# Opening stage of a diffusion trunk layer: conditioning product turned round, modulated tile in PSUM

## The chip, the cores and the metric

One core of one Trainium2 chip runs the kernel. The metric is the device time of one execution in microseconds (us). The kernel before took 2195.75 us in the median of three runs (2195.32 to 2199.14).

## The reference

One trunk layer runs on 1024 latent and 128 context tokens of 1024 channels in fp32. What matters here is its beginning:

```python
mod = silu(cond) @ ada_w + ada_b            # cond: two vectors (latent, context); ada_w is 1024 x 6144
sh1, sc1, g1, sh2, sc2, g2 = split(mod, 6)
h = rms_norm(x, n1_pre) * (1 + sc1) + sh1   # rms_norm: x * rsqrt(mean(x*x) + eps) * n1_pre
proj = h @ w_in                             # 1024 x 8192
```

After that come retention, a convolution branch, a merge and a convolutional feed-forward part. None of them is touched.

## The kernel before

A product in fp32 precision is made of three fp32r products: each operand is split into a high part (`A_hi`, `Wa_hi`) and a rest (`A_lo`, `Wa_lo`), and hi x hi, hi x lo and lo x hi are summed in PSUM. ScalarE makes the high part of a weight chunk (`split_w`) and GpSimd the rest.

All orders are written out by hand, one program for each engine, with semaphores between them. The opening stage goes so:

- SyncE loads `x` in three groups of three 128-token tiles, `ada_w`'s first 2048 columns in eight pieces of 256 columns (`ada_chunk`, 1 MB each), small rows, and chunks of `w_in` (`chunk_load`, 512 KB each), in one queue.
- TensorE multiplies each piece by the two conditioning vectors (`ada_early`): `cs` is the stationary operand (two columns), the piece moves. The result lies as two rows in PSUM. VectorE copies them to `mod_row` (`row_half`, L2188) and TensorE turns them into columns (`mod_turns`, L990, 16 turns of 2x128). VectorE adds the bias (`mod`) and forms `hscale`. The last piece comes behind the first eight of these turns and two `x_turn`.
- ScalarE squares the token tiles (`square`, L1450) and takes roots (`root`), VectorE forms the mean (`meaned`) and scales `x_all` (`normed`, L2184). In ScalarE's queue the squares of group 0 and 1 stand ahead of all modulated tiles, those of group 2 behind tile 7.
- There are 24 steps j = 8 g + k, one for each token group g (384 tokens) and 128-channel block k. TensorE turns three x tiles into one of three PSUM banks (`x_turn`, L1004). ScalarE scales and shifts the bank into one of six SBUF tiles `hf` (`modulated`, L1467). VectorE makes `A_hi` (L2197) and `A_lo` (L2198) from it (`halves`). In six of the steps ScalarE makes `A_hi` itself (`ON_ACT`).
- `first_u` on TensorE takes the 24 steps as they come: for each g first slot e = 0, whose step k waits for `A_lo` of j, then e = 1. `ahead` says how many `x_turn` stand ahead of each step. Behind it comes `q_half(0)`, the first product with 512 moving columns.

From step 3 on an `x_turn` waits until ScalarE has emptied the bank, and ScalarE's tile j waits for VectorE's j - 6, which frees its `hf` tile. Later in the kernel `ada_part` multiplies the other pieces of `ada_w` with the piece as stationary operand, strewn between other products. TensorE's products all have line L953, the helper `mm`.

Of the kernel before, what the change touches and what calls it, by code (L numbers as in the profile page):

```python
# [6 lines left out]
P = 128  # L7
D = 1024
# [55 lines left out]
def build(nc, a, out_xp, out_xs, out_sf, out_sb):  # L64
# [8 lines left out]
    with ctx:  # L73
# [56 lines left out]
        mod_row = at("mod_row", [2, 2 * D], a_at + 8 * KT * 2 * P * 4)  # L130
# [30 lines left out]
        hf = s0("hf", [P, 6, TG])  # L161
# [434 lines left out]
        ON_ACT = lambda j: j < 2 * KT and j % KT % 3 == 1  # L596
# [39 lines left out]
        def _(sp):  # L636
# [73 lines left out]
            ada_chunk(7)  # L710
            x_load(1)
            chunk_load(1)
# [238 lines left out]
        def _(pe):  # L951
# [28 lines left out]
            def ada_early(n):  # L980

                pe.wait_ge(ada_in[n % 4], 16 * (n // 4 + 1))
                for k in range(KT):
                    last = mm(ps[0:2, n // 2, (n % 2) * 256:(n % 2 + 1) * 256], cs[:, k, :], ada_p[:, n, k, :], k == 0, k == KT - 1)
                return last
            def mod_turns(half):

                pe.wait_ge(q.vec_ok, (2, 8)[half])
                for m in range(8 * half, 8 * half + 8):
                    pe.transpose(ps[:, 6, 2 * m:2 * m + 2], mod_row[0:2, m * P:(m + 1) * P], ident[0:2, 0:2]).then_inc(q.ada_used, 1)  # L990
            def x_turn(j):

                g, k = divmod(j, KT)
                if j == 0:
                    pe.wait_ge(q.vec_ok, 7)
                if j == 2:
                    pe.wait_ge(q.mod_ok, 1)
                if j >= 3:
                    pe.wait_ge(q.hT_f, j - 2)
# [17 lines left out]
            for n in range(8):  # L1017
                if n == 4:
                    row_turns()
                if n == 7:  # L1020
                    mod_turns(0)
                    x_turn(0)
                    x_turn(1)
                last = ada_early(n)
                if n % 4 == 3:
                    last.then_inc(q.vecT, 1)
            mod_turns(1)
            x_turn(2)


            def first_u():

                turned = 3
                pe.wait_ge(q.vec_ok, 8)
                for g in range(NTG):
                    for e in range(2):
# [6 lines left out]
                        for k in range(KT):  # L1043
                            ahead = KT * g + (k + 4 if e == 0 else 11 + (k // 2 if g else 0))
# [372 lines left out]
        def _(act):  # L1417
# [37 lines left out]
            def modulated(j):  # L1455
# [3 lines left out]
                if j >= 6:  # L1459
                    act.wait_ge(q.hT_lo, j - 5)  # L1460
                src, n = ps[:, TURN_BANK[j % 3], 0:TG], TG if g < 2 else 2 * P
                t3 = lambda x: x.rearrange("p (t n) -> p t n", n=P)
                outs = [t3(hf[:, j % 6, :])]
                if ON_ACT(j):
                    outs.append(A_hi[:, 3 * g:3 * g + 3, k, :])
# [7 lines left out]
            def squares(g):  # L1473

                for t in range(3 * g, 3 * g + 3):
                    square(t)
                root(g)
            squares(0)
            split_w(0)
            squares(1)  # L1480
            act.wait_ge(q.mod_ok, 2)
            for j in range(N_A):
                modulated(j)
                if j == 7:
                    squares(2)
                if j in (3, 15, 19, 21, 23):
                    split_w((3, 15, 19, 21, 23).index(j) + 1)
# [641 lines left out]
        def _(dve):  # L2129
# [55 lines left out]
            def row_half(n):  # L2185

                dve.wait_ge(q.vecT, (2, 8)[n])
                dve.tensor_copy(mod_row[:, n * D:(n + 1) * D].rearrange("c (b n) -> c b n", b=2),  # L2188
                                ps[0:2, 2 * n:2 * n + 2, :]).then_inc(q.vec_ok, 1)
            def halves(j):  # L2190
# [3 lines left out]
                h_ = hf[:, j % 6, :].rearrange("p (t n) -> p t n", n=P)  # L2194
# [9 lines left out]
            row_half(0)  # L2204
            dve.wait_ge(q.vecT, 7)
# [3 lines left out]
            row_half(1)  # L2209
            meaned(1)  # L2210
            dve.wait_ge(q.ada_used, 16)
            dve.wait_ge(q.vec_ok, 3)
            dve.tensor_tensor(mod[:, 0:16, :], ps[:, 6, 0:32].rearrange("p (k c) -> p k c", c=2), col2(V_ADAB, 16),
# [4 lines left out]
            for j in range(N_A):  # L2218
                if j == 3:
                    normed(1)  # L2220
                if j == 8:
                    meaned(2)
                    normed(2)
# [486 lines left out]
```

## Time and profile before

| | |
|---|---|
| median of the runs | 2195.75 us |
| the profiled execution | 2197.59 us |
| its span | 2195.8 us |
| TensorE busy (matmul) | 2142.4 us, 98% |
| VectorE / ScalarE / GpSimd busy | 1589.4 / 788.1 / 966.9 us |
| mean granted TensorE clock | 0.993 |

The profiled execution lies 1.8 us above its span. PE is the matmul side of TensorE, PEld its weight loads, DVE is VectorE, ACT is ScalarE, POOL is GpSimd, SP is SyncE. The granted clock is a share of 2.4 GHz; 0.50 is 1.2 GHz. The ends of matmuls are modelled, so the distance between two starts says more than a busy time.

### The profile page before, as it was taken

What the parts mean: (1) busy time and instruction counts of PE and PEld (TensorE: products, weight loads), DVE (VectorE), ACT (ScalarE), POOL (GpSimd) and SP (SyncE); (2) the same over time, 40 slices, a digit from 0 to 9 for tenths busy, and PEclk for the clock granted to TensorE, in tenths of its full rate; (3) what the DMA queues carried; (4) which work ended last, traced back from release to release, by engine and by line L of the source; (5) the groups of instructions that cost most, each with busy time, mean ns of one, the idle gap of its engine ahead of it and who ended that gap; (6) DMA issues with size and microseconds to landing.
All of it is one profiled execution on the core that took longest, in us unless ns stands there. A gap on an engine that the chain in (4) does not pass through costs nothing.

```text
span 2195.8 us, 31594 instructions
## 1 busy us (share of the span) xinstructions
PE 2142.4 (98%) x12483; PEld 1965.5 (90%) x12483; DVE 1589.4 (72%) x1790; ACT 788.1 (36%) x1326; POOL 966.9 (44%) x619
## 2 busy tenths in 40 slices
PE   7999999999999899999999999999999999999998
PEld 3888988988988899999899988889999999978886
DVE  3689589589489467676436536699898988766775
ACT  3401101101101266665548333343343333434342
POOL 1323323323323356665381220056656656565653
PEclk9999999999999999999999999999999999999999
DMA  9342442442432445545464344313232323375553
GB/s 304 111 128 95 129 128 87 133 128 81 131 106 88 156 153 164 167 147 158 153 219 146 125 168 141 99 35 87 63 88 61 91 61 91 107 296 183 201 181 128
DMA packets 246579, 291.79 MB, mean 133 GB/s; under 512 B 12225, under 2 KB 198945, under 8 KB 246433
## 3 DMA queue, kind: packets, MB, share of 16 engines
q1 hardware_dynamic: 178385, 221.33, 32.0%
q10 hardware_dynamic: 66640, 63.72, 8.9%
q0 software_dynamic: 1408, 4.72, 0.5%
q8 instruction: 100, 1.64, 0.3%
q14 instruction: 46, 0.38, 0.1%
HBM read 222.71 MB, written 67.01 MB: 132 GB/s over the span
## 4 chain that ended last, share of the span: by engine, by line
PE 90%; DVE 4%; DMA 2%; POOL 1%; ACT 1%; issue 1%; SPq 0%; ACTq 0%; DVEq 0%; POOLq 0%
PE ps L953 88%; DVE f_cv L2563 1%; DVE T_raw L2523 1%; PE ps L1163 1%; DMA ada_p<-in_ada_w 1%; DVE A_lo L2198 1%; POOL O_lo L2099 0%; DMA r_raw<-rT_d 0%; PE ps L1211 0%; DMA kv<-qkvg_d 0%; DMA sh_row<-gain_d 0%; DMA g_raw<-g_d 0%; DMA W_raw<-in_w_mix_out 0%; DVE A_hi L2197 0%; POOL f_cv L2104 0%
## 5 line engine op out<-in xcount | busy, mean ns | idle before, releaser
L2241 DVE SCALAR_TENSOR_TENSOR conv_y<-u_in,VC,conv_y 128x1167 f32<-128x1167 f32 x240 | 395.9, 1650 | 7.4
L1960 POOL TENSOR_TENSOR Wa_lo<-W_raw,Wa_hi 128x1024 fp32r<-128x1024 f32 x58 | 143.7, 2485 | 398.1 <-ACT Wa_hi L1419 398.0
L953 PE MATMUL ps<-A_hi,Wa_hi 128*128 128x384 f32 x768 | 271.8, 354 | 8.1 <-DVE A_lo L2198 7.3
L953 PE MATMUL ps<-A_hi,Wa_lo 128*128 128x384 f32 x768 | 259.6, 338 | 0.0
L953 PE MATMUL ps<-A_lo,Wa_hi 128*128 128x384 f32 x768 | 259.4, 338 | 0.0
L2563 DVE SCALAR_TENSOR_TENSOR f_cv<-f_in,VF,f_cv 128x1023 f32<-128x1023 f32 (+1 forms) x176 | 216.1, 1279 | 3.8 <-ACT f_cv L1847 2.1
L1960 POOL TENSOR_TENSOR D_lo<-F_raw,D_hi 128x1024 fp32r<-128x1024 f32 x66 | 162.3, 2463 | 100.0 <-ACT D_hi L1419 100.0
L2600 DVE TENSOR_TENSOR g_lo<-g_raw,g_hi 128x384 fp32r<-128x384 f32 x66 | 138.7, 2111 | 81.3 <-ACT g_hi L1419 81.3
L2099 POOL TENSOR_TENSOR O_lo<-E,O_hi 128x512 fp32r<-128x512 f32 x80 | 130.1, 1627 | 151.7 <-ACT O_hi L1419 151.7
L953 PE MATMUL ps<-Wb_hi,A_hi 128*128 128x512 f32 x432 | 179.7, 416 | 0.0
L2099 POOL TENSOR_TENSOR O_lo<-F_raw,O_hi 128x512 fp32r<-128x512 f32 x68 | 113.1, 1665 | 146.1 <-ACT O_hi L1419 146.1
L953 PE MATMUL ps<-Wb_hi,A_lo 128*128 128x512 f32 x432 | 170.7, 395 | 0.0
L953 PE MATMUL ps<-Wb_lo,A_hi 128*128 128x512 f32 x432 | 169.3, 392 | 0.0
L953 PE MATMUL ps<-D_hi,g_hi 128*128 128x512 f32 x396 | 155.2, 392 | 4.6 <-POOL D_lo L1960 2.4
L953 PEld LDWEIGHTS ps<-A_hi,Wa_hi 128*128 128x128 f32 x768 | 146.3, 190 | 11.5 <-DVE A_lo L2198 9.5
L953 PE MATMUL ps<-D_lo,g_hi 128*128 128x512 f32 x396 | 154.7, 391 | 0.0
L953 PE MATMUL ps<-D_hi,g_lo 128*128 128x512 f32 x396 | 154.6, 390 | 0.0
L1419 ACT ACTIVATE Wa_hi<-W_raw 128x1024 fp32r<-128x1024 f32 x58 | 60.6, 1056 | 259.2 <-DVE qk_st L2267 152.2
L953 PEld LDWEIGHTS ps<-A_lo,Wa_hi 128*128 128x128 f32 x768 | 146.3, 191 | 0.8
L953 PEld LDWEIGHTS ps<-A_hi,Wa_lo 128*128 128x128 f32 x768 | 145.6, 190 | 0.0
L953 PE MATMUL ps<-T_hi,O_hi 128*128 128x288 f32 x640 | 138.1, 298 | 4.5 <-ACT f_in L1419 4.0
L953 PE MATMUL ps<-B_hi,O_hi 128*128 128x288 f32 x608 | 140.9, 296 | 1.5 <-DVE B_lo L2509 1.0
(291 smaller groups left out, 5608.2 us busy)
## 6 DMA issues: line engine op xcount, KB each, us to landing
F_raw<-in_ffn_w_down SPq DMA_DIRECT2D x66, 512.0 KB, 3.6
F_raw<-in_ffn_w_up SPq DMA_DIRECT2D x44, 512.0 KB, 5.9
qt<-qkvg_d SPq DMA_DIRECT2D x36, 512.0 KB, 3.8
W_raw<-in_w_in SPq DMA_DIRECT2D x32, 512.0 KB, 5.1
W_raw<-in_w_in SPq DMA_DIRECT2D x64, 256.0 KB, 3.2
ada_w<-in_ada_w ACTq DMA_DIRECT2D x30, 512.0 KB, 4.3
g_d<-f_cv SPq DMA_DIRECT2D x22, 576.0 KB, 3.6
g_raw<-g_d SPq DMA_DIRECT2D x66, 192.0 KB, 3.6
```

The costliest lines, as they stand in the source:

```text
L953: return pe.matmul(out, l, r, start=start, stop=stop)
L1163: last = pe.transpose(ps[:, 2, x * P:(x + 1) * P], qt[:, n % 5, x // 2, (x % 2) * P:(x % 2 + 1) * P], ident[:, :])
L1419: return act.activation(dst, src, ACT.Copy)
L1960: return pool.tensor_tensor(dst, x, Fv(hi), ALU.subtract)
L2099: pool.tensor_tensor(O_lo[o % 4][:, :, :], op_src(o)[2], Fv(O_hi[o % 4][:, :, :]), ALU.subtract).then_inc(q.w_lo, 1)
L2198: dve.tensor_tensor(lo, h_, Fv(hi), ALU.subtract).then_inc(q.hT_lo, 1)
L2241: dve.scalar_tensor_tensor(out=y, in0=x, scalar=tap, in1=y, op0=ALU.mult, op1=ALU.add).then_inc(q.conv_step, 1)
L2523: dve.tensor_tensor(out, x, y, op).then_inc(q.t_ok, 1)
L2563: dve.scalar_tensor_tensor(out=f_cv[kind][:, o[0]:o[1]], in0=f_in[kind][:, x[0]:x[1]], scalar=VF[:, col:col + 1], in1=f_cv[kind][:, o[0]:o ...
L2600: dve.tensor_tensor(g_lo[c % 4][:, :], g_raw[c % 4][:, :], Fv(g_hi[c % 4][:, :]), ALU.subtract).then_inc(q.dg_lo, 1)
```

## The change

- `ada_early(n)` makes two 128-column blocks of the piece the stationary operand one after the other and moves `cs`, two columns. The result lies as columns in bank 0. `mod_row`, `row_half` and `mod_turns` go, and VectorE adds the bias straight from bank 0. All three first `x_turn` stand ahead of the last piece.
- `modulated(j)` writes back into its PSUM bank instead of `hf`; in `ON_ACT` steps it writes `A_hi` first. `halves(j)` reads the bank. `x_turn(j)` therefore waits for VectorE's part of j - 3.
- `ON_ACT` holds for k = 1 and 7 of the first two groups (four steps).
- The squares of groups 1 and 2 stand behind tiles 3, 4, 5 and 11, 12, 13, the roots behind 6 and 14. VectorE does `meaned` behind step 5 and 13 and `normed` behind step 7 and 15. The chunk split behind tile 3 stands behind tile 2.
- The turns ahead of each step of `first_u` change for group 0, both slots.
- SyncE loads chunk 1 ahead of the second x group.

```diff
@@ -593,7 +591,7 @@
 
         N_A = NTG * KT
         TURN_BANK = (5, 7, 6)
-        ON_ACT = lambda j: j < 2 * KT and j % KT % 3 == 1
+        ON_ACT = lambda j: j < 2 * KT and j % KT in (1, 7)
         def ada_unit_of(i, part):
 
             return 4 * i + part - 1 if i or part == 3 else None
@@ -708,8 +706,8 @@
                 ada_chunk(n)
             chunk_load(0)
             ada_chunk(7)
+            chunk_load(1)
             x_load(1)
-            chunk_load(1)
             sp.wait_ge(x_in[0], X_IN[0])
             x_load(2)
             sp.dma_start(x_all[:, NL, :], a["x_prompt"][0]).then_inc(x_in[2], 16)
@@ -980,23 +978,17 @@
             def ada_early(n):
 
                 pe.wait_ge(ada_in[n % 4], 16 * (n // 4 + 1))
-                for k in range(KT):
-                    last = mm(ps[0:2, n // 2, (n % 2) * 256:(n % 2 + 1) * 256], cs[:, k, :], ada_p[:, n, k, :], k == 0, k == KT - 1)
-                return last
-            def mod_turns(half):
-
-                pe.wait_ge(q.vec_ok, (2, 8)[half])
-                for m in range(8 * half, 8 * half + 8):
-                    pe.transpose(ps[:, 6, 2 * m:2 * m + 2], mod_row[0:2, m * P:(m + 1) * P], ident[0:2, 0:2]).then_inc(q.ada_used, 1)
+                for m in range(2 * n, 2 * n + 2):
+                    for k in range(KT):
+                        last = mm(ps[:, 0, 2 * m:2 * m + 2], ada_p[:, n, k, (m % 2) * P:(m % 2 + 1) * P], cs[:, k, :], k == 0, k == KT - 1)
+                    last.then_inc(q.ada_used, 1)
             def x_turn(j):
 
                 g, k = divmod(j, KT)
                 if j == 0:
-                    pe.wait_ge(q.vec_ok, 7)
-                if j == 2:
-                    pe.wait_ge(q.mod_ok, 1)
+                    pe.wait_ge(q.vec_ok, 6)
                 if j >= 3:
-                    pe.wait_ge(q.hT_f, j - 2)
+                    pe.wait_ge(q.hT_lo, j - 2)
                 if k == 0:
                     pe.wait_ge(q.xn_ok, 3 * g + 3)
                 b = TURN_BANK[j % 3]
@@ -1018,20 +1010,14 @@
                 if n == 4:
                     row_turns()
                 if n == 7:
-                    mod_turns(0)
-                    x_turn(0)
-                    x_turn(1)
-                last = ada_early(n)
-                if n % 4 == 3:
-                    last.then_inc(q.vecT, 1)
-            mod_turns(1)
-            x_turn(2)
+                    for j in range(3):
+                        x_turn(j)
+                ada_early(n)
 
 
             def first_u():
 
                 turned = 3
-                pe.wait_ge(q.vec_ok, 8)
                 for g in range(NTG):
                     for e in range(2):
                         slot = chunk_slot(e)
@@ -1041,7 +1027,9 @@
                         o = ps[:, 3 * e + g, 0:TG].rearrange("p (t n) -> p t n", n=P)
                         wh, wl = (x[slot].rearrange("p (k n) -> p k n", k=KT) for x in (w_hi, w_lo))
                         for k in range(KT):
-                            ahead = KT * g + (k + 4 if e == 0 else 11 + (k // 2 if g else 0))
+                            ahead = KT * g + (k + 4 if e == 0 else 11 + k // 2)
+                            if g == 0:
+                                ahead = min(k + 4, KT) if e == 0 else KT + (k + 1) // 2
                             while turned < min(ahead, N_A):
                                 x_turn(turned)
                                 turned += 1
@@ -1456,13 +1444,11 @@
 
                 g, k = divmod(j, KT)
                 act.wait_ge(q.hT_ps, j + 1)
-                if j >= 6:
-                    act.wait_ge(q.hT_lo, j - 5)
                 src, n = ps[:, TURN_BANK[j % 3], 0:TG], TG if g < 2 else 2 * P
                 t3 = lambda x: x.rearrange("p (t n) -> p t n", n=P)
-                outs = [t3(hf[:, j % 6, :])]
+                outs = [t3(src)]
                 if ON_ACT(j):
-                    outs.append(A_hi[:, 3 * g:3 * g + 3, k, :])
+                    outs.insert(0, A_hi[:, 3 * g:3 * g + 3, k, :])
                 for dst in outs:
                     ins = act.activation(dst[:, 0:n // P, :], t3(src)[:, 0:n // P, :], ACT.Identity,
                                          bias=mod[:, SH1 * KT + k, 0:1], scale=hscale[:, k, 0:1])
@@ -1470,21 +1456,20 @@
                         ins = act.activation(dst[:, n // P, :], src[:, n:TG], ACT.Identity,
                                              bias=mod[:, SH1 * KT + k, 1:2], scale=hscale[:, k, 1:2])
                 ins.then_inc(q.hT_f, 1)
-            def squares(g):
-
-                for t in range(3 * g, 3 * g + 3):
-                    square(t)
-                root(g)
-            squares(0)
+            for t in range(3):
+                square(t)
+            root(0)
             split_w(0)
-            squares(1)
             act.wait_ge(q.mod_ok, 2)
             for j in range(N_A):
                 modulated(j)
-                if j == 7:
-                    squares(2)
-                if j in (3, 15, 19, 21, 23):
-                    split_w((3, 15, 19, 21, 23).index(j) + 1)
+                g, k = divmod(j, KT)
+                if g < 2 and k in (3, 4, 5):
+                    square(3 * g + k)
+                if g < 2 and k == 6:
+                    root(g + 1)
+                if j in (2, 15, 19, 21, 23):
+                    split_w((2, 15, 19, 21, 23).index(j) + 1)
 
 
             def ada_load(x):
@@ -2182,16 +2167,11 @@
                 then(dve.reciprocal(rst[:, three], ssq[:, three]))
                 for t in range(3 * g, 3 * g + 3):
                     dve.tensor_scalar(x_all[:, t, :], x_all[:, t, :], rst[:, t:t + 1], None, ALU.mult).then_inc(q.xn_ok, 1)
-            def row_half(n):
-
-                dve.wait_ge(q.vecT, (2, 8)[n])
-                dve.tensor_copy(mod_row[:, n * D:(n + 1) * D].rearrange("c (b n) -> c b n", b=2),
-                                ps[0:2, 2 * n:2 * n + 2, :]).then_inc(q.vec_ok, 1)
             def halves(j):
 
                 g, k = divmod(j, KT)
                 dve.wait_ge(q.hT_f, j + 1)
-                h_ = hf[:, j % 6, :].rearrange("p (t n) -> p t n", n=P)
+                h_ = ps[:, TURN_BANK[j % 3], 0:TG].rearrange("p (t n) -> p t n", n=P)
                 hi, lo = (x[:, 3 * g:3 * g + 3, k, :] for x in (A_hi, A_lo))
                 if not ON_ACT(j):
                     then(dve.tensor_copy(hi, h_))
@@ -2201,27 +2181,23 @@
                 return V0[:, c:c + n].unsqueeze(2).broadcast_to([P, n, 2])
             meaned(0)
             normed(0)
-            row_half(0)
-            dve.wait_ge(q.vecT, 7)
+            dve.wait_ge(q.vecT, 6)
             for dst, src in ((V0[:, 16:120], ps[:, 7, 16:120]), (VF[:, 0:88], ps[:, 5, 0:88]), (VF[:, 88:176], ps[:, 5, 128:216]),
                              (VC[:, 0:124], ps[:, 4, 0:124]), (VC[:, 124:248], ps[:, 4, 128:252])):
                 dve.tensor_copy(dst, src).then_inc(q.vec_ok, 1)
-            row_half(1)
-            meaned(1)
             dve.wait_ge(q.ada_used, 16)
-            dve.wait_ge(q.vec_ok, 3)
-            dve.tensor_tensor(mod[:, 0:16, :], ps[:, 6, 0:32].rearrange("p (k c) -> p k c", c=2), col2(V_ADAB, 16),
+            dve.wait_ge(q.vec_ok, 2)
+            dve.tensor_tensor(mod[:, 0:16, :], ps[:, 0, 0:32].rearrange("p (k c) -> p k c", c=2), col2(V_ADAB, 16),
                               ALU.add).then_inc(q.mod_ok, 1)
             dve.wait_ge(q.mod_ok, 1)
             dve.scalar_tensor_tensor(out=hscale[:, :, :], in0=mod[:, SC1 * KT:SC1 * KT + KT, :], scalar=1.0,
                                      in1=col2(V_N1PRE, KT), op0=ALU.add, op1=ALU.mult).then_inc(q.mod_ok, 1)
             for j in range(N_A):
-                if j == 3:
-                    normed(1)
-                if j == 8:
-                    meaned(2)
-                    normed(2)
                 halves(j)
+                if j % KT == 5 and j < 2 * KT:
+                    meaned(j // KT + 1)
+                if j % KT == 7 and j < 2 * KT:
+                    normed(j // KT + 1)
 
 
             def taps_u(i, ws):
```

Left out of the diff: the allocations of `mod_row` and `hf`, which go.

## Rows read from the trace of the kernel before

**Rows 1.** Page, part 1: busy time, share of the span, instructions.
```profile
PE 2142.4 (98%) x12483; PEld 1965.5 (90%) x12483; DVE 1589.4 (72%) x1790; ACT 788.1 (36%) x1326; POOL 966.9 (44%) x619
```

**Rows 2.** Waits of PE, 44 to 95 us: us in total, times, longest.
```profile
PE ps L953 <- DVE A_lo L2198: 7.3, 6, 2.6
```

**Rows 3.** Chain of waits, 0 to 110 us: start, length, what.
```profile
20.20 7.17 PE ps L953 x32
...
28.00 10.45 PE ps L953 x48
...
39.84 3.56 PE ps L953 x16
...
43.42 1.22 DVE mod_row L2188
...
45.81 0.68 ACT hf L1467
...
57.28 0.64 PE ps L1004 x3
...
58.86 0.33 PE ps L1004 x3
...
60.04 4.69 PE ps L953 x27
...
86.56 23.53 PE ps L953 x112
```

**Rows 4.** Timeline of PE, 72 to 112 us: start, length.
```profile
92.66 0.39 PE L953 MATMUL ps<-Wa_hi,A_hi 128*128 128x512 f32 x1
```

**Rows 5.** Stretches: length; busy us PE, PEld, DVE, ACT, POOL; granted clock; DMA; GB/s.
```profile
45.00:48.00 3.00, 1.69 (x14) 1.16 (x14) 1.99 (x6) 2.49 (x7) 0.00 (x0) 1.00 1.06 364
48.50:51.50 3.00, 3.00 (x14) 2.81 (x12) 2.93 (x5) 2.87 (x5) 1.74 (x1) 0.50 0.66 208
79.00:82.00 3.00, 1.40 (x9) 1.16 (x9) 2.97 (x4) 1.12 (x3) 1.16 (x1) 1.00 0.00 0
```

**Rows 6.** Instructions on tile `ada_w`, 90 to 400 us: ns min/median/max.
```profile
L953 PEld LDWEIGHTS ps<-cs,ada_w x248: 187/188/189, 93.8 to 399.3; 128*128 128x128 f32 x124
```

**Rows 7.** Timeline of weight loads, 58.9 to 60.1 us: start, length.
```profile
58.92 0.19 PEld L953 LDWEIGHTS ps<-A_hi,Wa_hi 128*128 128x128 f32 x1
59.03 0.19 PEld L953 LDWEIGHTS ps<-A_lo,Wa_hi 128*128 128x128 f32 x1
```

**Rows 8.** Timeline of weight loads, 48.6 to 50.6 us.
```profile
48.64 0.34 PEld L953 LDWEIGHTS ps<-A_hi,Wa_hi 128*128 128x128 f32 x1
48.86 0.33 PEld L953 LDWEIGHTS ps<-A_lo,Wa_hi 128*128 128x128 f32 x1
```

**Rows 9.** Timeline of all engines, 0 to 62 us.
```profile
10.42 8.98 PE L953 MATMUL ps<-ada_p,cs 128*2 128x256 f32 x32 [6.23 <-DMA ada_p<-in_ada_w]
...
35.04 1.06 ACT L1419 ACTIVATE Wa_hi<-W_raw 128x1024 fp32r<-128x1024 f32 x1 [13.14 <-DMA W_raw<-in_w_in]
...
38.38 0.56 PEld L990 LDWEIGHTS ps<-ident,mod_row 2*128 2x128 f32 x8 [0.44 <-issue]
...
41.87 1.06 ACT L1450 ACTIVATE sq_t<-x_all 128x1024 f32<-128x1024 f32 x1 [5.77 <-DMA x_all<-in_x_sample]
```

**Rows 10.** Timeline of all engines, 98 to 105 us.
```profile
99.12 5.19 POOL L1960 TENSOR_TENSOR Wa_lo<-W_raw,Wa_hi 128x1024 fp32r<-128x1024 f32 x2 [2.17 <-ACT Wa_hi L1419]
...
99.67 0.88 DVE L2258 TENSOR_TENSOR rope_s<-ps,rope 128x128 f32<-128x128 f32 x4
...
100.58 1.48 DVE L2264 TENSOR_TENSOR qk_st<-rope_c,rope_s 128x512 f32<-128x512 f32 x1
```

**Rows 11.** Groups of DVE, 44 to 92.9 us: count, busy us, mean ns.
```profile
L2198 DVE TENSOR_TENSOR A_lo<-hf,A_hi 128x384 fp32r<-128x384 f32 x24 | 19.5, 825 | 1.1 <-ACT A_hi L1467 0.3
```

**Rows 12.** Timeline of all engines, 57 to 102 us.
```profile
61.39 2.08 DVE L2184 TENSOR_SCALAR x_all<-x_all,rst 128x1024 f32<-128x1024 f32 x3
...
65.49 0.56 DVE L2198 TENSOR_TENSOR A_lo<-hf,A_hi 128x384 fp32r<-128x384 f32 x1
```

More of the change, by code:

```diff
@@ L129, in build @@
         ada_p = at("ada_p", [P, 8, KT, 2 * P], a_at)
-        mod_row = at("mod_row", [2, 2 * D], a_at + 8 * KT * 2 * P * 4)
         kept = Region((rb_at, rb_at + 2 * act_bytes))
@@ L160, in build @@
         rows = s0("rows", [P, 5, P])
-        hf = s0("hf", [P, 6, TG])
         ssq = s0("ssq", [P, NT])
```

## The prediction

> **What bounds the kernel now.** The first view is the table of engines: TensorE is busy 98% of the span [rows 1]. The wait list of the opening says the same from the other side: between 44 and 95 us TensorE waited 7.3 us for `A_lo` [rows 2], and from 86.56 us it runs without a gap into the long stages [rows 3]. The change touches only what lies before that point, so its worth is how far it moves the instant at which TensorE leaves `first_u` (92.66 us, at the first 128x512 product [rows 4]). What is early there is early at the end, what is late is late, one for one.
>
> The second view is the chain of waits over the opening. From 20.20 us the conditioning products set it: 32, then 48, then 16 matmuls of `ps<-ada_p,cs` [rows 3], 0.22 us each (7.17 / 32), 16 for each of the eight 1 MB pieces of `ada_w`, so 3.56 us for a piece. Behind the last one come the row copy (1.22 us), eight small turns, and the two additions, until ScalarE starts the first modulated tile at 45.81 us [rows 3]. I call that instant S. `first_u` ends at S + 46.85.
>
> The third view is that of TensorE's granted clock in stretches [rows 5]; more on it below, since it decides the case.
>
> **Part 1: the conditioning product turned round.** Before, the stationary operand has two columns (`cs`) and 256 columns move. After, a 128x128 block of `ada_p` is stationary and two columns move. The kernel has this form already, later on: `ada_part` loads `ada_w` blocks as stationary operand for `cs`. Its row shows 248 weight loads of 188 ns busy in a stretch with 15.5 blocks of eight k, so two loads for each (block, k) [rows 6]. The change makes 16 blocks x 8 k x 2 = 256 weight loads with 256 two-column matmuls behind them. Two columns cost nothing; the loads are the price.
>
> How far apart do such loads start? At full clock two full loads that nothing holds back start at 58.92 and 59.03 us, 0.11 us apart [rows 7]; at half clock at 48.64 and 48.86 us, 0.22 us apart, and each is busy 0.33 us instead of 0.19 [rows 8]. So the load takes time with the clock. Lower bound for one load: 0.07 us, from eight loads of `mod_row` in 0.56 us at full clock [rows 9], but these are two rows high and belong to a transpose. Upper bound: 0.33 us, if at half clock each load had to end before its tiny matmul and the next load [rows 8]. I take 0.215 us, the half-clock spacing a little below its row, and now have to say why half clock.
>
> **The clock.** Between 45 and 48 us TensorE was busy 1.69 us and its weight loads 1.16 us, and in the next stretch the granted clock is 0.50, that is 1.2 GHz [rows 5]. Between 79 and 82 us it was busy less, 1.40 us with the same 1.16 us of loads, and the clock stayed at 1.00 (2.4 GHz) [rows 5]. [...] What differs is what ran: the first stretch was mostly two-column turns and transposes, the second mostly products with 384 columns. The conditioning stage after the change is nothing but loads and two-column products for its whole length. I expect it at 1.2 GHz from its first instruction to its last. Before, it began at half rate as well, but with 256 moving columns it came up after some 4 us (32 matmuls take 8.98 us from 10.42 us [rows 9], where 32 at full rate take 7.17 [rows 3]).
>
> The sum: TensorE starts at 10.42 us as before [rows 9]. 256 loads x 0.215 = 55.0 us. Eight pieces of 1 MB and more were in before 41.87 us [rows 9], so they come faster than one in 32 x 0.215 = 6.9 us, and from the second on no DMA wait remains. The five row turns cost 28.00 - (20.20 + 7.17) = 0.63 us now [rows 3], 1.2 us at half clock. Three `x_turn` now all stand ahead of the last piece: 0.64 us each at half clock [rows 3], 1.9 us. Behind the last piece only two additions stay, 0.45 us up to ScalarE's start. S = 10.42 + 55.0 + 1.2 + 1.9 + 0.45 = 69.0 us, against 45.81: **+23.2 us**. What the change removes there (the row copy with the turns behind it, 45.81 - 43.40 - 0.45 = 2.0 us [rows 3]) is already in this difference. The first copy and its eight turns go as well.
>
> The Trainium skill (TensorE: Matmul & The Clock Gate, section LDWEIGHTS) gives a load of 128 columns as 128 / 1.2, 107 ns, with no mention of the clock gate. The trace agrees at full clock and differs at half clock. By the rule alone the stage would take 256 x 0.107 = 27 us, as an estimate, and nothing would be lost; the same mechanism, priced from rows, is the first rival below.
>
> **Part 2: the modulated tile stays in PSUM.** VectorE's split reads PSUM instead of `hf`. Read from PSUM, a two-input operation is not slower: `rope_s<-ps,rope` ran 0.88 us for four while GpSimd was at work beside it from 99.12 us; `qk_st<-rope_c,rope_s` with both inputs in SBUF took 1.48 us there [rows 10]. This is the effect that makes 24 `A_lo` take 825 ns in the mean, 19.5 us [rows 11], where an undisturbed one takes 0.56 [rows 12]. So VectorE gets back up to 24 x 0.27 = 6.4 us, of which only what TensorE waits for counts. ScalarE's write into the same PSUM bank has no row; from below it is bounded by the 0.68 us that it takes from PSUM to SBUF [rows 3], from above I set double that, as for a bank read and written at once. I take 0.68, the only row near it, with 0.57 between starts.
>
> The price: `x_turn(j)` now waits for VectorE's part of j-3, not ScalarE's (six `hf` buffers are gone, three banks stay). Turn, ScalarE, VectorE together last some 2.5 us for three banks; VectorE alone needs about 1.06 us a step, so the banks are not what is late.
>
> **Part 3: squares and norms spread.** Here each instruction in the queues counts. With S as zero and full clock: step 0 to 2 as before, `A_lo` 0 done at 1.85. Then ScalarE splits W1 (1.05), and in each of the steps 3, 4, 5 does a tile (0.57) and a square (1.05 [rows 9]); TensorE gets step 7's operands at 11.0. `normed(1)` stands behind `halves(7)`, 0.2 + 2.1 us [rows 12], so turn 8 comes at 13.4, and TensorE waits a little over 1 us for it after one step of the second slot. Seven steps of three products (0.174 each, 4.69 / 27 [rows 3]) and four turns (0.33 each [rows 3]) later the first token group is done at 18.4. Before, it was done at 64.73 - 45.81 = 18.9 [rows 3].
>
> In the second group TensorE goes on to step 4 and wants turn 16 at 22.4. That turn needs `normed(2)`, which VectorE does after `halves(15)`, and ScalarE reaches tile 15 only after turn 11 (17.9) + tile 11 (0.7) + three squares with three tiles (4.9) + the root (0.3) + tile 15 twice (1.1) = 24.8; then 0.6 for the split and 2.4 for `normed(2)`: 27.8. So TensorE stands still from 22.4 to 27.8, **a new wait of 5.4 us**. Before, `normed(2)` began at 61.39 us [rows 12], long ahead of its turn, and this wait did not exist. From 27.8: three steps with two turns to 30.5, eight steps with three turns to 35.6, the third group 41.2 and 45.4. VectorE's two long stalls in that group are gone. Clock: at S it is low and stays so for the first steps, most of it under ScalarE's pace, 0.6 us; after 5.4 us of standing still it falls again, 1.7 us (half of one low stretch, as in [rows 5] from 48.5). `first_u` ends at S + 47.7, against 46.85: **+0.9 us**. The old waits (7.3 us [rows 2]) and the new ones cancel.
>
> W1 ahead of `x_load(1)` delays those rows by 0.5 MB, some 1.4 us, from 41.87 [rows 9]; the first of them is wanted at S + 4, long after. W0 arrived at 35.04 [rows 9], and W2 to W5 arrive in the idle time of the stage. All this is hidden. SP's queue waits for the last `A_lo` before it issues the next `ada_w` and rope tables, and that distance to their use stays about 6 us.
>
> The total is +24.1 us. The profiled execution took 2197.59 us, 1.8 above its span; with the change 2221.7. The median of the runs shown is 1.84 lower than the profiled one, so 2219.9 us.
>
> **Rivals.** (1) Not slower: the loads go at 0.11 us, because the clock is held or because loads do not follow it. A piece takes 3.5 us as before, the last ends at 43.4, S = 43.9, `first_u` +0.9: -1.0 us, 2194.7. For it: the full-clock row; TensorE never stands still in the stage. Against: [rows 8] and [rows 5]. The Trainium skill (same page, section Why this matters for your kernels) asks only that TensorE be kept busy, by which this is what would happen. The point from which it decides: at 0.13 us a load the gain is gone. (2) Faster: 0.07 us a load at full clock. Then the last piece's arrival is the bound, at about 38 us (1 MB behind W0 at 35.04), S = 38.0 + 2.3 + 0.45 = 40.8, and -5.0 + 0.4 gives 2191. Against: only a two-row load shows it. (3) Between: half clock, but part of the load hidden, 0.15 us: 38.4 us in place of 55.0, +7.5, 2203. (4) Worse: 0.33 us a load, 84.5 us, +53.6, 2249; against it, the loads of [rows 8] overlap.
>
> **The numbers.** Forecast 0.68, rival 1 0.14, rival 2 0.06, rival 3 0.08, rival 4 0.04. The forecast's own range is 2213 to 2228: loads at 0.21 to 0.23 us are -1.3 to +3.8, `first_u` may be 4 us better or 4 worse (double price of the PSUM write and the length of low clock above; all VectorE's gain counting below). The range for 8 in 10 takes in rival 3 and most of rival 1: 2194 to 2229. A change under 0.2%, 4.4 us, can't be told from none: 2191.4 to 2200.1. Faster: rival 2, 0.06. Same: rival 1, 0.14. Slower: 0.80.
>
> **What would show it.** The view of stretches must give a granted clock of 0.50 throughout 10 to 65 us (a first stretch may be unmarked), and weight loads of `ada_p` x256 with 0.33 us busy each. Loads busy 0.19 us mean rival 1. ScalarE's first tile should start near 69 us. Turn 16 should stand behind VectorE's normalisation of `x_all` for about 5 us, `A_lo<-ps` should be 0.56 us also beside GpSimd, and from then on nothing should differ. I am wrong if the clock is granted to loads alone.

## The result and the profile after

The changed kernel takes 2224.78 us in the median (2222.47 to 2228.40, 4 runs), the kernel before beside it 2195.53 us (2194.74 to 2199.14, 4 runs). The ratio is 1.0125, with a 95% interval of 1.0112 to 1.0138: **slower by 1.25%**, by the interval 25 to 30 us; the two medians lie 29.3 us apart. The profiled execution of the changed kernel took 2222.47 us with a span of 2220.6 us, against 2197.59 and 2195.8 before.

The table of engines after the change answers to [rows 1]:

```profile
PE 2165.2 (98%) x12595; PEld 2008.3 (90%) x12595; DVE 1584.1 (71%) x1790; ACT 786.3 (35%) x1324; POOL 965.7 (43%) x619
```

TensorE is still busy 98% and now for 22.8 us more, though two moving columns are next to no matrix work: each of the 256 new products stands as 353 ns of busy time in the median (below), while the next one starts after 0.21 us.

The chain of waits over the opening after the change (start, length in us, what) answers to [rows 3]:

```profile
9.53 27.44 PE ps L951 x128
37.98 20.28 PE ps L951 x96
58.25 2.02 PE ps L996 x9
60.28 6.63 PE ps L951 x32
67.37 0.64 ACT ps L1453
77.93 2.09 DVE x_all L2169 x3
92.22 4.17 DVE x_all L2169 x3
96.52 0.87 PE ps L996 x3
```

The conditioning products are one block of 128, one of 96 and one of 32, 54.35 us together, with only the row turns (1.0 us) and the three `x_turn` (2.0 us) between them. ScalarE starts the first modulated tile at S = 67.37 us; before it was 45.81 [rows 3].

All operations on the tile `ada_p` after the change (minimum, median and maximum duration in ns, first and last start in us) answer to [rows 6] and [rows 8]:

```profile
L951 PEld LDWEIGHTS ps<-cs,ada_p x256: 287/333/337, 9.5 to 66.5; 128*128 128x128 f32 x128
L951 PE MATMUL ps<-cs,ada_p x256: 213/353/353, 9.5 to 66.5; 128*128 128x2 f32 x128
```

The median load is busy 333 ns, the value that [rows 8] show at half clock (188 ns at full clock [rows 6]). They start 54.35 / 256 = 0.212 us apart.

The stretches of 10 us after the change (us, busy time and count of PE, PEld, DVE, ACT, POOL, then granted clock, DMA share, GB/s) answer to [rows 5]:

```profile
20.00:30.00 10.00, 10.00 (x48) 10.00 (x49) 2.25 (x4) 1.01 (x2) 0.00 (x0) 1.00 1.02 309
60.00:70.00 10.00, 7.55 (x38) 7.50 (x36) 2.28 (x6) 2.63 (x5) 0.00 (x0) 1.00 0.00 0
90.00:100.00 10.00, 3.48 (x14) 3.31 (x15) 7.08 (x10) 4.25 (x9) 2.61 (x1) 0.71 0.00 0
```

In the first row PE and PEld are busy without a gap, and the column of the granted clock says 1.00 while the loads inside last 333 ns. So this column doesn't mark the low clock of the opening. The first change that the trace records is a rise to 1.00 at 73.6 us, 6.3 us behind S, and the loads change there (timeline of weight loads, 67 to 76 us):

```profile
73.21 0.33 PEld L951 LDWEIGHTS ps<-A_lo,Wa_hi 128*128 128x128 f32 x1
74.15 0.19 PEld L951 LDWEIGHTS ps<-A_hi,Wa_hi 128*128 128x128 f32 x1
```

The durations and this first recorded rise are the evidence for the clock ahead of it.

Waits of TensorE between 60 and 125 us (engine and line, waited for: total us, times, longest) answer to [rows 2]:

```profile
PE ps L996 <- DVE x_all L2169: 8.1, 2, 7.1
PE ps L996 <- DVE A_lo L2178: 2.4, 1, 2.4
PE ps L951 <- DVE A_lo L2178: 1.3, 3, 0.8
```

The long wait is new: turn 16 stands behind VectorE's normalisation. What ran beside that stands in the timeline from 91 us (start, length, engine, line, operation):

```profile
92.22 4.16 DVE L2169 TENSOR_SCALAR x_all<-x_all,rst 128x1024 f32<-128x1024 f32 x3
92.55 2.61 POOL L1945 TENSOR_TENSOR Wa_lo<-W_raw,Wa_hi 128x1024 fp32r<-128x1024 f32 x1 [19.43 <-ACT Wa_hi L1407]
96.52 0.87 PE L996 MATMUL ps<-ident,x_all 128*128 128x128 f32 x3 [7.12 <-DVE x_all L2169]
```

These normalisations took 2.08 us before [rows 12], and those of the second group 2.09 us at 77.93 us in the chain above; here they took twice that beside GpSimd's 2.61 us. The Trainium skill (GPSIMD Engine Reference, section 1. Specifications) says that GpSimd shares its SBUF interfaces with VectorE and contends when VectorE runs in a two-port mode or has two inputs in SBUF. The trace agrees with the contention: the three one-input normalisations of SBUF data doubled from 2.08 to 4.17 us. With one input only the two-port condition could apply to them, and in which mode they ran no view shows.

VectorE's and ScalarE's tiles between 60 and 125 us (count | busy us, mean ns | idle before) answer to [rows 11]:

```profile
L2178 DVE TENSOR_TENSOR A_lo<-ps,A_hi 128x384 fp32r<-128x384 f32 x24 | 13.4, 557 | 1.6 <-ACT ps L1453 0.8
```

```profile
L1453 ACT ACTIVATE ps<-ps,mod,hscale 128x384 f32<-128x384 f32 x16 | 10.3, 650 | 34.8 <-DVE hscale L2193 30.4 <-PE ps L996 4.4
```

The split fell from 825 ns [rows 11] to 557 ns in the mean, and ScalarE's write into the bank that it reads costs 650 ns, no more than the 0.68 us into SBUF [rows 3].

Last, the mark of the stage's end, the first product with 512 columns, answers to [rows 4]:

```profile
116.48 0.39 PE L951 MATMUL ps<-Wa_hi,A_hi 128*128 128x512 f32 x1
```

It lies at S + 49.1. Before, it lay at S + 46.85 [rows 4]. So the opening lost 21.6 us up to S and 2.3 us behind it, 23.8 in all; the span lost 24.8.

### The profile page after: what moved, and what is told of

It reads as the page before. It is cut to its first block, busy times and chain, and to the rows that moved or that the text cites. A ratio compares the mean times of both kernels' runs of the same rounds, so it can differ in the third digit from the quotient of the medians.

```text
span 2220.6 us, 31798 instructions
## 1 busy us (share of the span) xinstructions
PE 2165.2 (98%) x12595; PEld 2008.3 (90%) x12595; DVE 1584.1 (71%) x1790; ACT 786.3 (35%) x1324; POOL 965.7 (43%) x619
## 4 chain that ended last, share of the span: by engine, by line
PE 87%; DVE 5%; DMA 3%; ACT 3%; POOL 1%; issue 1%; SPq 0%; ACTq 0%; DVEq 0%; POOLq 0%
PE ps L951 85%; DVE f_cv L2539 1%; DMA gate_t<-gate_d 1%; DVE T_raw L2499 1%; PE ps L1151 1%; ACT c_raw L1729 0%; DMA kv<-qkvg_d 0%; DMA ada_p<-in_ada_w 0%; DMA r_raw<-rT_d 0%; PE ps L1199 0%; DVE c_raw L2436 0%; ACT ps L1453 0%; DMA xt<-in_x_prompt 0%; PE ps L996 0%; ACT sq_t L1438 0%
```

## The experiments

Two theories of the loss. **Clock**: the conditioning stage runs at 1.2 GHz because nothing but loads and two-column products runs in it; each load costs 0.21 us. **Rivals**: the loss is a price of loads as such, or comes from other parts (squares, PSUM tile, order of loads). The first piece of `ada_w` arrives at another time in each profiled execution, and TensorE's stage starts between 9.5 and 11.5 us with it, so part of a difference in S, 1 us or more, can be that arrival. "First tile" in the table is S, and "behind it" is the distance from S to the first 512-column product, in the profiled execution.

| kernel | median us (runs) | before beside it | ratio, 95% | first tile | behind it |
|---|---|---|---|---|---|
| before | | | | 45.81 | 46.9 |
| changed | 2224.78 (4) | 2195.53 | 1.0125, 1.0112 to 1.0138 | 67.37 | 49.1 |
| changed, again | 2225.51 (4) | 2197.85 | 1.0121, 1.0104 to 1.0138 | 67.66 | 49.5 |
| rows_back | 2200.04 (10) | 2196.66 | 1.0021, 1.0012 to 1.0030 | 46.78 | 48.6 |
| cond_only | 2221.63 (4) | 2196.66 | 1.0115, 1.0098 to 1.0131 | 69.10 | 46.9 |
| wide128 | 2200.35 (10) | 2196.66 | 1.0015, 1.0005 to 1.0025 | 45.09 | 48.4 |
| wide32 | 2225.04 (4) | 2196.66 | 1.0131, 1.0116 to 1.0147 | 68.95 | 49.0 |
| loads_twice | 2281.61 (2) | 2197.85 | 1.0381, 1.0361 to 1.0402 | 123.22 | 48.9 |
| split_late | 2221.73 (2) | 2197.49 | 1.0113, 1.0074 to 1.0151 | 68.36 | 47.2 |
| psum_only | 2193.48 (12) | 2197.82 | 0.9985, 0.9976 to 0.9994 | 46.04 | 41.5 |
| early2_wide | 2191.52 (12) | 2197.82 | 0.9980, 0.9971 to 0.9990 | 43.73 | 40.2 |
| early2_turns | 2191.51 (10) | 2197.82 | 0.9976, 0.9967 to 0.9985 | 43.81 | 40.2 |
| early2_rows | 2191.40 (11) | 2197.82 | 0.9975, 0.9966 to 0.9983 | 46.84 | 40.2 |

### rows_back: the change with the conditioning product of before

```diff
-                for m in range(2 * n, 2 * n + 2):
-                    for k in range(KT):
-                        last = mm(ps[:, 0, 2 * m:2 * m + 2], ada_p[:, n, k, (m % 2) * P:(m % 2 + 1) * P], cs[:, k, :], ...)
+                for k in range(KT):
+                    last = mm(ps[0:2, n // 2, (n % 2) * 256:(n % 2 + 1) * 256], cs[:, k, :], ada_p[:, n, k, :], ...)
...
+            mod_row, mod_turns and row_half as before
```

> The kernel after with the conditioning product put back to two stationary columns and 256 moving ones; the PSUM tile and the spread squares stay. Theory (the loss is the conditioning stage at half clock): ScalarE's first tile starts at 45 to 46.5 us again, first_u lasts 48 to 50 us from there, 2196 to 2199 us, so 1 to 3 us above the kernel before, because of the stall ahead of turn 16. Rival (the new schedule of squares and norms carries much of the loss): above 2205 us. Second rival (VectorE's regained 6 us count): 2190 us.

The chain of waits in its opening:

```profile
28.90 10.52 PE ps L952 x48
40.81 3.56 PE ps L952 x16
46.78 0.65 ACT ps L1466
```

and TensorE's wait between 40 and 125 us:

```profile
PE ps L1003 <- DVE x_all L2182: 8.1, 2, 7.1
```

The stage is back at its old pace and 3.4 us (the ratio says 0.21%) of the loss are left, with the same 7.1 us wait as in the changed kernel. The median of 2200.04 lies 1 us above the range expected for it. So the rest of the change, taken together, costs a little, and the conditioning product the rest.

### cond_only: the kernel before with the turned product alone

```diff
+                for m in range(2 * n, 2 * n + 2):
+                    for k in range(KT):
+                        last = mm(ps[:, 0, 2 * m:2 * m + 2], ada_p[:, n, k, (m % 2) * P:(m % 2 + 1) * P], cs[:, k, :], ...)
...
-            mod_row, mod_turns, row_half; hf, squares and turns stay as before
```

> The kernel before with the conditioning product turned round and nothing else. Theory: 256 weight loads 0.214 us apart, first tile near 67.4 us instead of 45.8, first_u as long as before or up to 3 us shorter since x and the squares of two groups are ready; 2214 to 2218 us. Rival (the parts only hurt together): under 2205 us.

Its operations on `ada_p`:

```profile
L952 PEld LDWEIGHTS ps<-cs,ada_p x256: 287/333/337, 11.2 to 68.2; 128*128 128x128 f32 x128
```

and its first product with 512 columns:

```profile
115.97 0.39 PE L952 MATMUL ps<-Wa_hi,A_hi 128*128 128x512 f32 x1
```

The same loads, and S + 46.9 as in the kernel before. The median is 25.0 us above the one beside it, 1.7 us more than the difference in S (23.3), and at 2221.63 it is 3.6 us above the top of the expected range. The profiled execution can't explain that: it took 2231.40 us, 9 to 11 more than the other three, and its trace shows 6 us of this in a late stretch at half clock (below, with the total). The two runs say the same from both sides: undoing the product takes nearly all of the loss away, doing it alone brings nearly all of it.

### wide128 and wide32: the same loads with more columns to move

```diff
-                        last = mm(ps[:, 0, 2 * m:2 * m + 2], ada_p[...], cs[:, k, :], ...)
+                        last = mm(ps[:, m // 4, (m % 4) * P:(m % 4 + 1) * P].rearrange("p (r c) -> p r c", c=2), ada_p[...],
+                                  cs[:, k, :].unsqueeze(1).broadcast_to([P, 64, 2]), ...)
```

The two columns of `cs` are read 64 times over (16 times in wide32), so each product moves 128 (32) columns, and VectorE picks the first two.

> The kernel after with cs repeated 64 times as moving operand, 128 columns instead of 2, of which two are used: 64 times the streaming work with the same 256 weight loads. Theory (weight loads don't hold the clock, moving columns do): after a cold beginning of some 4 us the granted clock is 1.00, loads are busy 0.19 us and start 0.11 us apart, the first tile starts at 43 to 46 us, 2196 to 2202 us. Rival (the loads take 0.214 us of themselves, by their fp32 data or beside the DMA traffic, whatever the clock): more work makes it no faster, 2222 us or more.

> As wide128 with 32 moving columns. Theory: too little streams, the clock stays at 1.2 GHz, loads 0.214 us apart as with 2 columns, 2222 to 2227 us. If a quarter of the width is enough to hold the clock: 2196 to 2202 us. The rival that loads take 0.214 us of themselves gives 2222 to 2227 too, so this run tells only together with wide128.

Operations on `ada_p` in wide128, and the end of its stage in the chain of waits:

```profile
L951 PEld LDWEIGHTS ps<-cs,ada_p x256: 186/191/333, 10.6 to 44.2; 128*128 128x128 f32 x128
```

```profile
29.08 10.98 PE ps L951 x96
41.05 3.59 PE ps L951 x32
45.09 0.64 ACT ps L1454
```

Operations on `ada_p` in wide32, and the start of its stage, at the pace of the changed kernel:

```profile
L951 PEld LDWEIGHTS ps<-cs,ada_p x256: 287/333/337, 11.0 to 68.0; 128*128 128x128 f32 x128
```

```profile
11.07 27.48 PE ps L951 x128
```

The two runs together settle the theory. With 64 times the columns the stage ends over 22 us earlier (S 45.09 against 67.37), since its loads now last 191 ns and start 0.11 us apart (10.98 / 96 and 3.59 / 32). With 16 times the columns nothing changes. The first recorded change of the granted clock, to 1.00, comes at 15.8 us in wide128, and at 75.0 us in wide32, as late as in the changed kernel. The number, size and place of the loads are the same in all three kernels, and wide32 spreads its results over the same four banks as wide128, so the loss is no price of loads or of banks as such but the clock at which the loads run. Between 32 and 128 columns I ran nothing. The whole of wide128 is still 3.7 us behind the kernel before: its first 512-column product, at 93.52 us, is 0.9 later, and the rest comes later on (below, with the total).

### loads_twice: each two-column product issued twice

```diff
+                    for k in range(KT):
+                        mm(ps[:, 1, 2 * m:2 * m + 2], ada_p[:, n, k, (m % 2) * P:(m % 2 + 1) * P], cs[:, k, :], ...)
```

> The kernel after with each two-column product of the conditioning stage issued a second time, into an unused bank. Theory (a load of 128 columns costs 0.214 us at 1.2 GHz and nothing else counts): 512 loads, first tile 256 x 0.214 = 54.9 us later, near 122 us, about 2279 us. Rival (the price is a fixed one of the stage or of its DMA): much less.

Its operations on `ada_p`, and ScalarE's first tile:

```profile
L951 PEld LDWEIGHTS ps<-cs,ada_p x512: 288/333/338, 10.7 to 122.3; 128*128 128x128 f32 x171
```

```profile
123.22 0.64 ACT L1455 ACTIVATE ps<-ps,mod,hscale 128x384 f32<-128x384 f32 x1 [85.17 <-DVE hscale L2195]
```

The first tile comes 55.6 us later than in the changed kernel beside it (67.66). Of that 1.0 us is the first piece, whose products start at 10.77 instead of 9.81 us. The products themselves take 108.96 us (54.74, 40.76 and 13.46 in the chain of waits) instead of 54.35, so 256 loads more cost 54.6 us: 0.213 us each. That is the price of one load at 1.2 GHz, measured as a difference, with every other part of the stage unchanged. Another 55 us of uninterrupted loads did not raise the clock either.

### split_late: the weight split away from the norm

```diff
-                if j in (2, 15, 19, 21, 23):
-                    split_w((2, 15, 19, 21, 23).index(j) + 1)
+                if j in (2, 17, 19, 21, 23):
+                    split_w((2, 17, 19, 21, 23).index(j) + 1)
```

> The kernel after with the split of weight chunk 2 behind tile 17 instead of 15, so that GpSimd doesn't work beside normed(2). Theory (the norm's 4.17 us in place of 2.08 is that neighbour): normed(2) takes 2.1 us, TensorE's wait for x_all ahead of turn 16 shrinks from 7.1 to about 5.1 us, the first 128x512 product comes 1.5 to 3 us earlier after the first tile. Rival (the norm is slow for another reason, for instance x_all's address): 4.2 and 7.1 us as before.

Its wait and its normalisations between 40 and 125 us:

```profile
PE ps L996 <- DVE x_all L2169: 6.0, 2, 5.0
```

```profile
L2169 DVE TENSOR_SCALAR x_all<-x_all,rst 128x1024 f32<-128x1024 f32 x6 | 4.2, 750 | 0.1
```

With GpSimd's `Wa_lo` two tiles later the three normalisations take 2.08 us, the wait falls from 7.1 to 5.0 us, and the distance behind S from 49.1 to 47.2. So 2.1 of the 7.1 us are GpSimd beside the norm, and the other 5.0 are put down to the order of the squares and the norm, which early2_wide below moves. The interval of its ratio overlaps that of the changed kernel; only the trace tells the two apart.

### psum_only: the kernel before with the tile in PSUM alone

```diff
-                outs = [t3(hf[:, j % 6, :])]
+                outs = [t3(src)]
...
-                    pe.wait_ge(q.hT_f, j - 2)
+                    pe.wait_ge(q.hT_lo, j - 2)
```

> The kernel before with the modulated tile kept in PSUM and nothing else. Theory (a split that reads PSUM isn't slowed by GpSimd): A_lo 0.56 us in the mean instead of 0.825, TensorE's waits for A_lo in the third group (4.1 us) nearly gone, first_u 42 to 44.5 us instead of 46.85, 2191 to 2194 us. Rival (three banks instead of six tiles cost as much as that gives): 2196 us.

VectorE between 40 and 125 us:

```profile
L2195 DVE TENSOR_TENSOR A_lo<-ps,A_hi 128x384 fp32r<-128x384 f32 x24 | 13.1, 556 | 1.3 <-ACT ps L1464 0.7
```

This part gains by itself: the distance behind S falls from 46.9 to 41.5, and the ratio is 0.9985. The 5.4 us of distance and 4.3 us of time are a gain that the prediction had only as a bound (up to 6.4). So three banks in place of six tiles held nothing up that cost more than this. In the changed kernel `A_lo` is as fast (557 ns), and the new wait of turn 16 took the gain back: the distance is 48.6 in rows_back, which has the 7.1 us wait, and 41.5 here.

### early2_wide, early2_turns, early2_rows: squares of the third group moved forward

```diff
-                if g < 2 and k in (3, 4, 5):
-                    square(3 * g + k)
+                if g == 0 and k in (3, 4, 5):
+                    square(k)
...
+                if j == 7:
+                    for t in (6, 7, 8):
+                        square(t)
+                    root(2)
```

VectorE does `meaned(2)` behind `normed(1)` and `normed(2)` behind step 8. early2_wide has the product of wide128, early2_turns has it too with the three first `x_turn` behind the last piece, early2_rows has the product of before.

> The kernel with 128 moving columns in the conditioning product, and the squares, the root and the norm of the third token group moved forward: squares 6 to 8 behind tile 7, normed(2) behind halves(8). Theory (the stall ahead of turn 16, 7.1 us, is caused by where the squares and the norm stand in the two queues): the stall goes, and with it the stretch at half clock behind it; first_u lasts 40 to 42 us instead of 48.4, so 7 us less than with wide128 alone, about 2193 us, under the kernel before. Rival (three banks of PSUM are too few, and the wait only moves to the tiles): first_u 46 us or more, 2198 us.

> As early2_wide with the first three x_turn behind the last conditioning piece instead of ahead of it, beside VectorE's two additions. Theory: the first tile starts 0.7 to 1 us earlier, the rest as it was, 2192 us. Rival: the piece waits for its DMA then, nothing gained.

> As early2_wide, but with the conditioning product as in the kernel before (two stationary columns, row copy, turns). Theory: first tile at 45.8 to 46.8 us against 45.1, first_u 40 to 42 us; 2193 to 2195 us, so the turned product is worth 1 to 2 us once its clock is held.

In early2_wide, TensorE's waits between 40 and 125 us and the two marks of the stage:

```profile
PE ps L997 <- DVE A_lo L2183: 3.3, 3, 2.4
PE ps L951 <- DVE A_lo L2183: 1.9, 4, 0.8
PE ps L997 <- DVE x_all L2174: 1.0, 1, 1.0
```

```profile
43.73 0.64 ACT L1454 ACTIVATE ps<-ps,mod,hscale 128x384 f32<-128x384 f32 x1 [6.41 <-DVE hscale L2198]
...
83.92 0.39 PE L951 MATMUL ps<-Wa_hi,A_hi 128*128 128x512 f32 x1
```

Turn 16 no longer waits, and `first_u` ends 40.2 us behind S instead of 48.4. All three beat both kernels, by 0.20 to 0.25% against the one before. They can't be told from one another, though S is 3.1 us later in early2_rows (46.84) than in early2_wide (43.73). Of that, 1.2 us are the arrival of the first piece (the products start at 11.5 and 10.3 us); in the profiled executions the later steps described below take back the rest. I had expected the turned product to be worth 1 to 2 us once its loads run at full clock; the medians (2191.52 and 2191.40) show nothing of it, and with intervals of some 2 us to each side a gain of 1 us can be neither shown nor excluded. Putting the turns behind the last piece (early2_turns) was expected to bring S 0.7 to 1 us forward and gave nothing: S is 43.81 against 43.73. They no longer stood in the way of the last piece, but the fifth one came late in that execution:

```profile
28.65 14.69 PE L951 MATMUL ps<-cs,ada_p 128*128 128x128 f32 x128 [1.18 <-DMA ada_p<-in_ada_w]
```

The bracket of this line of TensorE's timeline is the idle time ahead of it: 1.18 us of waiting for the piece, about the 1.0 us that the turns had cost.

## Why the prediction was right, step by step

- **The rate of the loads** (forecast 0.215 us at half clock): measured 0.212, and 0.213 by loads_twice. This step carries the case. It came from two rows: two loads 0.22 us apart [rows 8], and the pair of stretches with equal load time of which only one kept the clock [rows 5]. The second of the two is a thin support, and here the forecast had some luck. The trace of the kernel before has a third stretch, which the prediction doesn't show:

```profile
82.60:86.00 3.40, 1.59 (x6) 0.95 (x6) 3.33 (x5) 2.34 (x3) 2.27 (x1) 1.00 0.00 0
86.00:89.40 3.40, 2.85 (x9) 2.85 (x10) 0.50 (x1) 1.13 (x1) 2.18 (x2) 0.50 0.48 133
```

  TensorE ran nothing but products with 384 columns there, and the clock fell behind it all the same. So the pair alone doesn't show that the kind of work decided; the runs with 2, 32 and 128 columns do, for a stage in which TensorE hardly stands still (not at all with 2 and 32 columns, 1.1 us for a piece in wide128).
- **Half clock for the whole stage**: shown by 333 ns loads from 9.5 to 66.5 us, the first recorded rise at 73.6 us, and by wide128. The sign that the prediction named first, a granted clock of 0.50 in the view of stretches, did not come: the view says 1.00 throughout, not only in a first stretch. The second sign, 0.33 us a load, did. Rival 1 (not slower) rested on the clock being held while TensorE never stands still; it never stood still, and the clock wasn't held. The Trainium skill (TensorE: Matmul & The Clock Gate, section Why this matters for your kernels) advises keeping TensorE busy without gaps to get and keep the full clock. The runs differ for this kind of work: busy for the whole 10 us stretch from 20 us with 333 ns loads, and the same with 32 columns. Rivals 2 to 4 (0.07, 0.15 and 0.33 us a load) fall with the 0.212. The point at which rival 1 puts the gain at nothing, 0.13 us a load, isn't what the forecast's own sum gives: 24.1 us are 0.094 us for each of 256 loads, and 0.215 less 0.094 is 0.12.
- **S**: forecast 69.0, measured 67.37. The stage began at 9.53 instead of 10.42, the turns took 1.0 instead of 1.2, the loads 54.35 instead of 55.0. The 0.9 us of the start are the arrival of the first piece and not the change's.
- **Turn 8**: forecast a little over 1 us of standstill, measured 1.0.
- **Turn 16**: forecast 5.4 us, measured 7.1. The term that I left out is GpSimd's `Wa_lo` beside `normed(2)`: I had put 2.1 us for the three normalisations, and they took 4.17. I had counted what GpSimd does to the two-input split of the tile and not asked the same of the one-input norm. The trace of the kernel before already had the row, for `normed(1)`, just ahead of the window of [rows 12] (timelines of VectorE and GpSimd):

```profile
49.48 4.19 DVE L2184 TENSOR_SCALAR x_all<-x_all,rst 128x1024 f32<-128x1024 f32 x3
49.76 2.69 POOL L1960 TENSOR_TENSOR Wa_lo<-W_raw,Wa_hi 128x1024 fp32r<-128x1024 f32 x1 [11.23 <-ACT Wa_hi L1419]
```

  split_late gives 5.0 us without it, close to the forecast. The terms up to tile 15 add up to 24.9 and not 24.8, which changes nothing.
- **The clock behind it**: I set a low stretch priced at 1.7 us. It was granted 1.2 GHz for 6.8 us from 94.1 us on, twice the length that I had priced, but TensorE stood still for the first 2.4 of them, until 96.52.
- **`A_lo` and the PSUM write**: forecast 0.56 and 0.68 us, measured 0.557 and 0.650.
- **`first_u`**: forecast S + 47.7, measured S + 49.1. The missed norm is 2.1 of it; the rest of the sum came out 0.7 shorter and isn't resolved further.
- **The total**: forecast +24.1 us on the profiled execution, measured 2222.47 - 2197.59 = 24.9. "What is early there is early at the end, one for one" was too simple. The starts of the same matmul in two kernels, counted from the last one back, show where the distance changes (us later than in the kernel before, in the profiled executions, each counted from the start of its span):

| kernel | up to about 750 us | behind 780 us | 1480 to 1800 us | last matmuls |
|---|---|---|---|---|
| changed | 24.2 | 26.2 | 27.1 | 24.8 |
| changed, again | 24.7 | 27.5 | 28.8 | 28.6 |
| cond_only | 23.4 | 25.5 | 34.5 | 33.6 |
| rows_back | 2.7 | 4.1 | 3.1 | 2.5 |
| wide128 | 1.2 | 4.8 | 5.4 | 4.9 |
| psum_only | -4.6 | -2.1 | -3.0 | -3.1 |
| early2_wide | -8.5 | -6.5 | -5.0 | -5.2 |
| early2_rows | -5.3 | -6.9 | -6.7 | -8.7 |

The distance is constant over hundreds of us, then takes a step at the same few pieces of work. At the first such place, before and after, TensorE's waits for `kb_lo` (total, times, longest) are

```profile
PE ps L953 <- POOL kb_lo L1960: 4.9, 3, 2.9
```

```profile
PE ps L951 <- POOL kb_lo L1945: 6.2, 3, 4.2
```

and the granted clock behind them (the last but two columns hold it), again before and after, is

```profile
765.30:768.70 3.40, 3.40 (x14) 3.40 (x13) 1.14 (x2) 0.00 (x0) 0.00 (x0) 0.50 0.22 77
```

```profile
769.90:776.70 6.80, 4.72 (x17) 4.75 (x18) 2.05 (x3) 2.00 (x5) 1.45 (x2) 0.50 0.60 189
```

Twice as long at half clock and 1.3 us more of waiting: that is the step from 24.2 to 26.2. At the end it goes the other way, since the kernel before is granted half clock from 1932.7 to 1936.1 us and the changed one isn't. In cond_only a stretch stands where the kernel before has none, behind a 4.1 us wait for `X_lo`, and its distance grows by about 6 us there:

```profile
1342.50:1349.30 6.80, 5.11 (x12) 4.05 (x13) 0.15 (x1) 2.07 (x3) 1.63 (x1) 0.52 0.06 25
```

- **The median** is 4.9 us above the forecast. The two profiled executions lie on opposite sides of their medians (before 2.1 above, changed 2.3 below), so the medians are 29.3 us apart where the traces are 24.9. Steps as in the table, of 1 to 6 us and different between two executions of one kernel (24.8 and 28.6 at the end), are large enough for that. The changed kernel, run again, was to tell the two apart: a difference of the medians of 24 to 26 us if the later stages add nothing, 27 to 30 if their steps last. It came out at 27.7 us, but with an interval of 23 to 30, which takes in both. The executions behind the medians have no trace, so this remains a reading. Open is also whether the wait for `kb_lo` follows from the change: it is 4.9, 5.4, 6.4 and 4.9 us in the four kernels with the product of before (before, rows_back, psum_only, early2_rows) and 5.7 to 7.0 us in the nine traces with the turned one. No run tried it.

## What to carry to other kernels

Turning a thin product so that the weights become the stationary operand trades columns for full loads; if the loads run at 1.2 GHz, price them at 0.21 us a 128x128 load, not 0.11. In these runs TensorE was 100% busy with such loads for 57 us and stayed at 1.2 GHz, with 2 and with 32 moving columns, and went to 2.4 GHz within 6 us with 128. Repeating columns that nobody needs made the stage as short as before, not shorter, so what gained here was the tile in PSUM together with the place of the squares and norms. Read the clock of an opening stage from the durations of its loads (0.19 or 0.33 us), since the clock column didn't mark it here. When a step of VectorE is moved, look at what GpSimd will be doing at its new place, for its one-input SBUF operations too, and follow the last of the spread pieces to the turn that needs it.

## What the runs showed of the hardware that was not expected

- More columns can make a stage shorter: 256 products with 128 columns ended 22 us before the same 256 with 2 columns, at 191 instead of 333 ns a load. The prediction had no such run; the expectation written for it had this.
- With 32 columns the stage stayed as it was: 333 ns a load, the same as with 2 columns, and the first recorded rise at 75.0 us.
- A clock column of 1.00 stood over 57 us of loads at half clock (333 ns).
- Three normalisations of 128x1024 in SBUF, one input each, took 4.17 us beside 2.61 us of GpSimd's two-input operation, and 2.08 us alone. VectorE's two-input operation with one input in PSUM kept its 557 ns in the mean over 24.
